# Values of two heads in one matmul of 256 columns, with the even head's banks and the rotation's buffers reassigned

## What is computed

```python
h = rmsnorm(x, g_pre_mix)
z = h @ w_in
b_g, c_g, xin, cq, ckv_raw, kpe_raw, ga, gb = jnp.split(z, [...], axis=-1)
yc, new_buf = short_conv(c_g * xin, conv_buf, conv_w)
y_a = b_g * yc
q = (rmsnorm(cq, g_q) @ w_uq).reshape(B, L, N_HEADS, QK_DIM)
q_nope, q_pe = q[..., :QK_NOPE], apply_rope(q[..., QK_NOPE:], cos, sin)
ckv_new = rmsnorm(ckv_raw, g_kv)
k_nope = jnp.einsum('bkc,chd->bkhd', ckv, w_uk.reshape(KV_LORA, N_HEADS, QK_NOPE))
v = jnp.einsum('bkc,chd->bkhd', ckv, w_uv.reshape(KV_LORA, N_HEADS, V_DIM))
s = (einsum(qn, k_nope) + einsum(qp, kpe)) * SM_SCALE      # masked, softmax -> p
y_b = jnp.einsum('bhqk,bkhd->bqhd', p, v)
merged = jax.nn.sigmoid(ga) * y_a + jax.nn.sigmoid(gb) * y_b
x = x + rmsnorm(merged @ w_o, g_post_mix)
x = x + rmsnorm(jnp.square(jax.nn.relu(rmsnorm(x, g_pre_ffn) @ w1)) @ w2, g_post_ffn)
```

## Time and profile before

| | us |
|---|---|
| median of 3 runs | 1858.07 (1856.78 to 1858.64) |
| the profiled execution | 1856.37 |
| its span, from first to last instruction | 1854.6 |
| TensorE busy in it | 1825.9 |
| VectorE busy | 1081.4 |
| ScalarE busy | 655.4 |

### The profile page before, as it was taken

How to read it: one execution, slowest core, us unless ns; L and a number is a source line. 1 busy time by engine, 2 the same in 40 slices (tenths; PEclk the granted TensorE clock), 3 DMA queues, 4 the chain that set the end, 5 groups by cost and what they waited for, 6 DMA issues and landing times. The chain is left out here.

```text
span 1854.6 us, 31641 instructions
## 1 busy us (share of the span) xinstructions
PE 1825.9 (98%) x13604; PEld 1804.7 (97%) x13604; DVE 1081.4 (58%) x2096; ACT 655.4 (35%) x1242; POOL 13.6 (1%) x20
## 2 busy tenths in 40 slices
PE   7999999999999999999999999999999999999997
PEld 7999999999999999999999999999999999999996
DVE  6655555556674455556587555555557725555555
ACT  6634343434452222222265343434435512222221
POOL 0100000000000000000010000000000000000000
PEclk9999999999999999999999999999999999999998
DMA  4322222221112322222122212121312212222221
GB/s 165 110 74 71 75 70 75 71 103 58 68 50 80 135 73 76 80 92 92 58 99 75 79 65 81 64 82 63 112 47 94 80 42 108 91 92 92 71 67 52
DMA packets 43658, 149.69 MB, mean 81 GB/s; under 512 B 4864, under 2 KB 8960, under 8 KB 43520
## 3 DMA queue, kind: packets, MB, share of 16 engines
q1 hardware_dynamic: 42784, 146.17, 22.8%
q10 hardware_dynamic: 736, 1.51, 0.2%
HBM read 143.80 MB, written 3.87 MB: 80 GB/s over the span
## 5 line engine op out<-in xcount | busy, mean ns | idle before, releaser
L519 PE MATMUL ring<-xs_hi,w_lo 128*128 128x288 f32 x2752 | 820.3, 298 | 11.2 <-DVE w_lo L1276 9.6
L521 PE MATMUL ring<-xs_hi,w_hi 128*128 128x288 f32 x2752 | 812.3, 295 | 0.0
L520 PE MATMUL ring<-xs_lo,w_hi 128*128 128x288 f32 x2752 | 811.9, 295 | 0.0
L519 PEld LDWEIGHTS ring<-xs_hi,w_lo 128*128 128x128 f32 x2752 | 517.6, 188 | 14.4 <-issue 10.8
L520 PEld LDWEIGHTS ring<-xs_lo,w_hi 128*128 128x128 f32 x2752 | 517.7, 188 | 1.5
L521 PEld LDWEIGHTS ring<-xs_hi,w_hi 128*128 128x128 f32 x2752 | 517.3, 188 | 0.0
L1276 DVE TENSOR_TENSOR w_lo<-w_raw,w_hi 128x1024 fp32r<-128x1024 f32 x236 | 286.0, 1220 | 95.7 <-ACT w_hi L945 54.4
L519 PE MATMUL att<-f_hi,w_lo 128*128 128x288 f32 x1024 | 302.3, 295 | 0.5 <-DVE w_lo L1276 0.5
L520 PE MATMUL att<-f_lo,w_hi 128*128 128x288 f32 x1024 | 301.8, 295 | 0.0
L521 PE MATMUL att<-f_hi,w_hi 128*128 128x288 f32 x1024 | 301.7, 295 | 0.0
L722 ACT ACTIVATE w_hi<-w_raw 128x1024 fp32r<-128x1024 f32 x156 | 159.3, 1048 | 106.4 <-DMA w_raw<-blocks_in 106.2
(11 more groups left out here) (228 smaller groups left out, 2103.1 us busy)
## 6 DMA issues: line engine op xcount, KB each, us to landing
w_raw<-blocks_in SPq DMA_DIRECT2D x236, 512.0 KB, 3.3
small_raw<-small_in SPq DMA_DIRECT2D x10, 768.0 KB, 5.0
small_raw<-small_in SPq DMA_DIRECT2D x8, 576.0 KB, 4.8
x<-x_in SPq DMA_DIRECT2D x8, 288.0 KB, 7.3
kv_out<-kv ACTq DMA_DIRECT2D x2, 576.0 KB, 3.4
x_out<-x SPq DMA_DIRECT2D x1, 1152.0 KB, 5.0
x_out<-x SPq DMA_DIRECT2D x4, 288.0 KB, 2.2
cache_t_raw<-cache_t_in SPq DMA_DIRECT2D x2, 512.0 KB, 5.9
```

The source lines that it names most:

```text
L519: pe.matmul(out, w[1], x[0], start=first, stop=False)
L520: pe.matmul(out, w[0], x[1], start=False, stop=False)
L521: return pe.matmul(out, w[0], x[0], start=False, stop=last)
```

## The change

The value weights of both heads of a pair lie side by side in `small` (columns `SV` to `SPE`), and in an even head the values of both heads are made together: for each of four token tiles and two latent chunks three matmuls with 256 moving columns, two token tiles to a bank (`values(0)` into bank 1536, `values(1)` into bank 0). An odd head makes only its keys. `v` holds both heads and the last product picks the head's half.

Since bank 0 is now taken by values, the even head's query goes to banks 512 and 1024 (`query_tile`). So in an even head `values(1)` waits for the rotation's first half, the query's first half for the second, and its second half for the keys' low part (`proj_lo`). `k_hi` and `k_lo` stand ahead of the rotary parts in ScalarE's and VectorE's queues.

`rope_t` and `rope_s` share the memory of `cv` and `u`, so ScalarE waits for the former head's `merged` ahead of the rotation. `ybt` is gone: the attention part is written to `my` at once, block 4 is multiplied into `ga`, and the two are added. The block 4 product of the second half is two operations (224 and 64 columns) in place of one. `context_s` of the sample stage lies on the prompt's latents.

An even head's small weights come in five transfers (`even_small`; 1792 columns), an odd head's in two (`odd_small`; 896), counted by `small_in`.

In the first head of a layer (`first`) VectorE splits the weights of blocks 3 and 4 and of the next head's first two blocks later: one behind the normalised probabilities, three behind `probs_t_lo`.

```diff
+SQ, SK, SKT, SV, SPE = 0, 384, 640, 896, 1408
+SME, SMO, SMV = 1792, 896, 1024
+SMALL_DMAS = [5, 2] * (HEADS // 2) + [1, 1]
...
+        self.sh, self.sl, self.sraw = split("small", [P, SME], raw=True)
...
+        self.vh, self.vl = split("v", [P, KT, 2, P])
...
+        turn = mark[0]
         self.cv = put("cv", [P, NT + 2])
         self.u = put("u", [P, NT + 4])
-        self.ybt = put("ybt", [P, NP_])
+        after_head, mark[0] = mark[0], turn
         self.rope_t, self.rope_s = put("rope_t", [P, 2, NH]), put("rope_s", [P, 2, NH])
+        assert mark[0] <= after_head
...
+        mark[0] = latents
+        self.och, self.ocl = split("context_s", [P, CC, P])
+        assert mark[0] <= latents + 4 * NP_
...
+def small_in(L, n):
+
+    return 16 * (L * sum(SMALL_DMAS) + sum(SMALL_DMAS[:n + 1]))
+
+
+def small_width(n):
+    return SMV if n >= HEADS else SMO if n % 2 else SME
...
+        def even_small(L, p):
+            both = small[L * 5 + p]
+            values = pl.sraw[:, SV:SPE].rearrange("p (c h d) -> p c h d", c=CC, h=2)
+            sp.dma_start(pl.sraw[:, 0:SKT], both[:, 0:UV]).then_inc(pl.small_landed, 16)
+            sp.dma_start(pl.sraw[:, SKT:SV], both[:, UKT:UPE]).then_inc(pl.small_landed, 16)
+            for h in range(2):
+                of_h = both[:, SWE * h + UV:SWE * h + UKT].rearrange("p (c d) -> p c d", c=CC)
+                sp.dma_start(values[:, :, h, :], of_h).then_inc(pl.small_landed, 16)
+            sp.dma_start(pl.sraw[:, SPE:SME], both[:, UPE:SWE]).then_inc(pl.small_landed, 16)
+
+        def odd_small(L, p):
+            of_h = small[L * 5 + p][:, SWE:SWE + SWO]
+            sp.dma_start(pl.sraw[:, 0:SKT], of_h[:, 0:UV]).then_inc(pl.small_landed, 16)
+            sp.dma_start(pl.sraw[:, SKT:SMO], of_h[:, UKT:UPE]).then_inc(pl.small_landed, 16)
...
+            even_small(L, 0)
...
+                                odd_small(L, p)
+                            elif p < HEADS // 2 - 1:
+                                even_small(L, p + 1)
...
-        def small_hi(L, j, n, more=0):
-            eng.wait_ge(pl.small_landed, (L * 10 + (j + 1) + more) * 16)
+        def small_hi(L, j):
+            n = small_width(j)
+            eng.wait_ge(pl.small_landed, small_in(L, j))
...
+                    def keys_hi():
                         projected(2)
                         act.activation(pl.kh[:, :], pl.att[:, 1024:1536], ACT.Copy).then_inc(pl.proj_hi, 1)
-                        projected(3)
-                        act.activation(pl.vh[:, :], pl.att[:, 1536:2048], ACT.Copy).then_inc(pl.proj_hi, 1)
+
+                    def values_hi(two):
+                        projected(3 + two)
+                        act.activation(pl.vh[:, 2 * two:2 * two + 2, :, :], value_tiles(pl, two), ACT.Copy) \
+                            .then_inc(pl.proj_hi, 1)
...
+                        else:
+                            eng.wait_ge(pl.merged, L * HEADS + p * 2)
                         for half in range(2):
                             projected(half)
                             rope_halves(pl.att[:, 512 * half:512 * half + NH], pl.rope_s[:, half, :], pl.rope_swapped)
                             if p == 0:
                                 key_hi(half)
+                        keys_hi()
...
-                        keys_values_hi()
+                        values_hi(0)
+                        values_hi(1)
                         query_hi()
...
+                        keys_hi()
...
+def query_tile(pl, e, half):
+
+    at = 512 * (half + (1 - e))
+    return pl.att[:, at:at + NH]
+
+
+def value_tiles(pl, two):
+
+    at = (1536, 0)[two]
+    return pl.att[:, at:at + 512].rearrange("p (k h d) -> p k h d", k=2, h=2)
...
+                    def gated_out(src, half):
+                        if half == 0:
+                            dve.tensor_tensor(pl.ga[:, 0:NH], src, pl.ga[:, 0:NH], ALU.mult).then_inc(pl.ring_free, 1)
+                        else:
+                            dve.tensor_tensor(pl.my[:, p * 2 + e, NP_:NT], src[:, NP_ - NH:NH], pl.ga[:, NP_:NT],
+                                              ALU.mult)
+                            dve.tensor_tensor(pl.ga[:, NH:NP_], src[:, 0:NP_ - NH], pl.ga[:, NH:NP_], ALU.mult) \
+                                .then_inc(pl.ring_free, 1)
+
+                    def merge(k, t, sem):
+                        eng.wait_ge(pl.pv_read, L * HEADS + k + 2)
+                        dve.tensor_tensor(pl.my[:, k, t], pl.my[:, k, t], pl.ga[:, t], ALU.add).then_inc(sem, 1)
...
+                    def keys_lo(j):
                         proj_lo(j, pl.kl[:, :], pl.att[:, 1024:1536], pl.kh[:, :])
-                        proj_lo(j + 1, pl.vl[:, :], pl.att[:, 1536:2048], pl.vh[:, :])
+
+                    def values_lo(two):
+                        tiles = slice(2 * two, 2 * two + 2)
+                        proj_lo(1 + two, pl.vl[:, tiles, :, :], value_tiles(pl, two), pl.vh[:, tiles, :, :])
 
                     def first_gate():
                         head_out(pl.gb[:, cols(0)], 0, 0, pl.rx)
                         head_out(pl.gb[:, cols(1)], 0, 1, pl.rx)
-                        next_weight(0)
+                        if not first:
+                            next_weight(0)
+
+                    first = p == 0 and e == 0
...
+                        keys_lo(0)
...
-                        keys_values_lo(0)
-                        query_lo(2)
+                        values_lo(0)
+                        values_lo(1)
+                        query_lo(3)
...
                             weight_lo(L, n_head(0, 2), SLOT_HD[2])
-                            weight_lo(L, n_head(0, 3), SLOT_HD[3])
...
-                        keys_values_lo(2)
+                        keys_lo(2)
...
-                    next_weight(1)
+                    if not first:
+                        next_weight(1)
...
+                    if first:
+                        weight_lo(L, n_head(0, 3), SLOT_HD[3])
                     head_out(pl.cv[:, cols(1)], 2, 1, pl.rx2)
-                    next_weight(2)
+                    if not first:
+                        next_weight(2)
...
+                    if first:
+                        next_weight(0)
+                        next_weight(1)
+                        next_weight(2)
+                    small_lo(p * 2 + e + 1)
...
+                    dve.scalar_tensor_tensor(out=pl.my[:, k, 0:NP_], in0=pl.gb[:, 0:NP_], scalar=1.0,
                                              in1=pl.att[:, 1024:1536], op0=ALU.add, op1=ALU.mult) \
                         .then_inc(pl.pv_read, 1)
...
                     if k < HEADS - 1:
-                        for half in range(2):
-                            src = entry(4, half)
-                            dve.tensor_tensor(pl.my[:, k, cols(half)], src, pl.ga[:, cols(half)], ALU.mult) \
-                                .then_inc(pl.ring_free, 1)
+                        gated_out(entry(4, 0), 0)
+                        gated_out(entry(4, 1), 1)
                         own_ring(4, 1)
-                        dve.tensor_tensor(pl.my[:, k, 0:NP_], pl.my[:, k, 0:NP_], pl.ybt[:, :], ALU.add) \
-                            .then_inc(pl.merged, 1)
+                        merge(k, slice(0, NP_), pl.merged)
...
-                        out = att[:, 512 * half:512 * half + NH]
+                        out = att[:, 512 * half:512 * half + NH] if at == SPE else query_tile(pl, e, half)
...
+                    def values(two):
+
+                        tiles = value_tiles(pl, two)
+                        for kt in range(2):
+                            at = P * (2 * two + kt)
                             for c in range(CC):
-                                last = mm3(pe, att[:, 1536 + P * kt:1536 + P * (kt + 1)], rows_of(ckv, ALL, c, keys),
-                                           small_w(UV, c), c == 0, c == CC - 1)
+                                last = mm3(pe, tiles[:, kt, :, :], rows_of(ckv, ALL, c, slice(at, at + P)),
+                                           rows_of(small, ALL, slice(SV + 2 * P * c, SV + 2 * P * (c + 1))),
+                                           c == 0, c == CC - 1)
                         last.then_inc(pl.projected, 1)
...
-                        keys_values()
-                        for half in range(2):
-                            eng.wait_ge(pl.rope_sum, p * 2 + (L * 8 + half + 1))
-                            query(UQ, half)
+                        keys()
+                        values(0)
+                        eng.wait_ge(pl.rope_sum, p * 2 + (L * 8 + 1))
+                        values(1)
+                        eng.wait_ge(pl.rope_sum, p * 2 + (L * 8 + 2))
+                        query(SQ, 0)
+                        eng.wait_ge(pl.proj_lo, L * 32 + p * 8 + 1)
+                        query(SQ, 1)
                     else:
-                        query(UQ, 0)
-                        query(UQ, 1)
-                        keys_values()
```

(6 more changed lines are left out.)

73 lines of the change are left out of this document (26 added, 47 removed).

## The result

| | before | after |
|---|---|---|
| median of the runs, us | 1857.46 (1856.78 to 1858.64, 4 runs) | 1831.74 (1831.14 to 1834.77, 4 runs) |
| profiled execution, us | 1856.37 | 1832.2 |
| its span, us | 1854.6 | 1830.4 |

The ratio is 0.9864, with a 95% interval of 0.9847 to 0.9881: 22 to 28 us less. A second set of runs of both kernels, on another occasion, gave 1832.71 against 1856.57, ratio 0.987 (0.9855 to 0.9886).

The account below looks back on a forecast made before the run. TensorE, busy 1825.9 of 1854.6 us, was taken as the bound. Terms -21.4 + 1.6 + 0.2 - 3.0 = -22.6 us took the span to 1832.0 and the median from 1858.07 to 1835.5 us, range 1833.0 to 1841.0.

Parts of the forecast that it names:

- Odd heads, -21.4: Value matmuls leave the 8 odd heads, taking 2.68 us each off TensorE's line: -21.4 us.
- even heads, +1.6: In 8 even heads, 24 value matmuls of 256 columns at 0.12 us cost 0.20 us more a head: +1.6 us.
- rival (b): Even heads' 256-column value matmuls cost 0.17 us each instead of 0.12, ending at 1845.5 us; chance 0.04.
- some 10 us: Total saving on value matmuls by the Trainium skill's rule, 1.3 us a pair of heads instead of 2.5.
- New waits, +0.2: TensorE's waits for rotation and low keys cost 0 in later even heads, 0 to 0.1 in 2 first heads: +0.2 us.
- The margins 0.55 and 1.0: In an even head the rotation ends 0.55 us and the low keys 1.0 us before TensorE needs them.
- Rival (a): Rotation or keys come 0.5 to 1.0 us late in each even head, 4 to 8 us, 1839.5 to 1843.5; chance 0.08.
- First heads, -3.0: In each layer's first head, moving three weight splits behind the softmax removes the transposes' wait for probabilities: -3.0 us.
- What is late next: First heads' third-block weight split, 1.22 us, now follows the probabilities directly; claimed ready within 0.1 us of need.
- Rival (c): First heads keep their wait because another operation in VectorE's queue is as late, 1838.5 us; chance 0.06.
- Loads, 0: Extra small-weight transfers land in time and wider copies and splits stay hidden: cost 0.
- rival (d): The five small-weight transfers land late and delay TensorE's product with the values, about 1864 us at 18 us landing; chance 0.02.

Follow-up runs that it names:

- keys_late: Changed kernel with an even head's low keys made behind the low halves of the rotary query parts on VectorE: 1843.24 us against 1832.71.
- one_load: Changed kernel with small weights laid out by the host, so each head's load is one transfer instead of five or two: 1833.68 us.
- narrow_last: Kernel before, with only the small weights' copy and split behind each layer's last head cut from 1536 to 1024 columns: 1855.55 us, ratio 0.9997.
- wide_last: Changed kernel with each layer's last small load, copy and split 1536 columns wide again: 1833.4 us, beside 1832.71 in another set.

## Why the prediction was right, and where it was not

**Odd heads, -21.4; even heads, +1.6.** Right to 0.01 us a head in the trace (-2.68, and +0.20 in six even heads; what the two first ones cost above that is the next term), and the experiment that undoes the width alone gives back 19.9 us of the 19.8. The choice of 0.12 for 256 columns, from the distance inside a run of them, was right; rival (b) with 0.17 fell. The rule of the Trainium skill that was weighed there ("TensorE: Matmul & The Clock Gate", section "Back-to-back issue gap", 81 ns at 128 columns) doesn't hold for these matmuls: 0.109 at 128 stationary columns. The same page's section "LDWEIGHTS (loading the stationary operand)" makes the load proportional to the stationary columns; the 0.060 at 64, about half, agrees with that. The 109 ns for 256 columns that the prediction set beside the 81 is the page's figure for a matmul by itself, not for a stream of weight loads and matmuls, so its saving of "some 10 us" mixed two kinds of figure; the trace shows 0.12.

**New waits, +0.2.** Right: nothing in six even heads, some 0.09 and 0.12 us in the two first ones, though the list of waits shows none. The margins 0.55 and 1.0 came out as 0.46 and 1.06. Rival (a) did not happen, but keys_late shows it as a real mechanism, with a price above what (a) gave: one operation moved costs 10.5 us.

**First heads, -3.0.** Right: -1.53 and -1.47 in the trace, -3.0 alone. "What is late next", the split for the third block, did cost nothing. Rival (c) fell.

**Loads, 0.** The transfers did cost nothing, shown by one_load, and rival (d) fell. (Its price was mis-added: by the prediction's own figures a landing at 18 us would give about 1868, not 1864.) The copies and splits behind them are item 2 below.

**The part that the traces can price** is 23.4 us, where the sum said 22.6: 0.8 us off, most of it item 2 below. The rest of the miss is in how the sum was turned into a median.

**What failed, in the order of size.** The forecast was 3.8 us too high (1835.5 - 1831.74). The steps that failed are the one from the span to the median, which took one set's chance offset over as if it were the kernel's, and the "Cost 0" of the small copies and splits.

1. "Of the profiled span: 1854.6 to 1832.0 ... from which I take the same" (the 1.7 us between profiled execution and median). The new span was 1.6 lower than this sum (-0.65 of item 2 below, -1.5 of the clock stretch, +0.7 of the first load; the rest is rounding), and the new median lay 0.5 *below* its profiled execution, where I had added 1.7: 1.6 + 2.2 = 3.8. The median of three runs that I started from was itself high: in three later sets the kernel before had 1856.57, 1856.45 and 1856.17. And the profiled execution of before held one stretch at the 1.2 GHz level, that of after none. Each profiled execution is its kernel's own time plus 0, 1.5 or 3 us, plus up to 1.6 for the first load. Which of them a set of four runs catches is luck: the changed kernel's second set had 1832.71 with the same code.
2. "The wider copy and split ... hidden; the odd ones shrink" and "Cost 0". That was read in one head in the middle of a layer, and holds there. But the last head's split shrinks too, from 1536 to 1024 columns, and it stands at the front of a VectorE row without slack that TensorE waits for twice: -0.92 us, shown by narrow_last and wide_last. And the split for layer two's first head, wider by 256 columns, stands right ahead of `cqn_lo`: +0.27 us. The term should have been -0.65 us. Both rows were in the list of waits (`xs_lo`, 0.4 us, 2 times; `cqn_lo`, 0.3 us, once), but I read only waits in the middle of the heads.

The range reached 2.5 us below the forecast and 5.5 above. Above stood the rivals; below I had put only the spacing and "the runs' spread (1.9)", though the scatter of before and after both count and lie on both sides. With the scatter that the runs show, 1831.74 was within reach even of the sum as it stood: 1832.0 + 1.8 for what lies outside the span, less 1.5 for the stretch and 0.7 for an earlier first load, is 1831.6.

## What to carry to other kernels

In a run of them, a matmul cost here the longer of its stationary load and its moving stream. Where a stream of matmuls with 128 stationary columns starts 0.109 us apart, up to 192 moving columns were free and 256 cost a tenth more, so look for two narrow products with the same stationary operand. When a bottleneck engine has few waits, check every one against every operation that the diff shortens or lengthens, those too that seem to lie beside the path: what counts is whether the queue between them has slack. And before a median is predicted from one profiled execution, look for what in it is chance, here the first load and stretches at the lower clock, and let the range reach below by as much as above.

## What the runs showed of the hardware

The distance from start to start, all with 128 stationary columns and at the 2.4 GHz level: 0.109 us for 128 moving columns, 0.11 for 192, 0.12 for 256, 0.133 for 288, 0.175 for 384, 0.235 for 512; with 64 stationary and 128 moving columns, 0.060. Below 128 moving columns it falls no further: with 64 of them it is 0.111 in the median of the kernel before. From 256 to 512 that is 0.115 us for 256 columns; taken down in proportion it would give 0.062 for 128, an estimate, close to the 0.060 that was seen once the load was halved.

Between its first matmuls and its last one the granted clock fell to 0.50 for between 3 and 4 us once or twice in 8 of 12 profiled executions and in the others not at all, each time in the sample tokens' attention, where matmuls of 512 columns follow ones of 128, with TensorE busy right before it. What decides whether it falls was not found; its price of 1.5 us is larger than several of the terms that a prediction of this kind is made of.
